# First column of the first projection: two weight tiles times the first 528 tokens in plain fp32, tile by tile as the rows come

## The reference

```python
h = rms_norm(x, norm_pre[0])              # 1056 tokens x 1024
proj = h @ w_in[0]                        # 1024 -> 4 * 1024
v, bg, cg, z = jnp.split(proj, 4, axis=-1)
u = cg * v
conv = w_conv[0] * u_ext[:, 0:T] + ...    # three taps over time
y = (bg * conv * jax.nn.silu(z)) @ w_out[0]
x = x + rms_norm(y, norm_post[0])
```

## Time and profile before

| | us |
|---|---|
| median of 3 runs | 1091.33 |
| lowest, highest | 1090.86, 1092.24 |
| the profiled execution | 1090.71 |
| its span, first to last instruction | 1089.0 |

### The profile page before, as it was taken

How to read it: one execution, slowest core, us unless ns; L and a number is a source line. 1 busy time by engine, 2 the same in 40 slices (tenths; PEclk the granted TensorE clock), 3 DMA queues, 4 the chain that set the end, 5 groups by cost and what they waited for, 6 DMA issues and landing times.

```text
span 1089.0 us, 20411 instructions
## 1 busy us (share of the span) xinstructions
PE 1066.0 (98%) x7995; PEld 1002.6 (92%) x7995; DVE 723.7 (66%) x1294; ACT 386.5 (35%) x738; POOL 38.8 (4%) x53
## 2 busy tenths in 40 slices
PE   6999999999999999999999999999999999989997
PEld 6999999999999888799999999999999999967885
DVE  6798677677678546645657495875849587485146
ACT  7443333333335344433142331414233241532123
POOL 1000000000000000001001010100101010010000
PEclk9999999999999999999999999999999999999999
DMA  6102221211121542122202211210221121121143
GB/s 223 38 20 78 58 60 39 57 58 39 58 58 58 168 144 98 64 64 58 59 23 59 61 48 48 60 55 25 58 60 41 56 60 46 54 77 60 42 178 121
DMA packets 93317, 74.30 MB, mean 68 GB/s; under 512 B 2519, under 2 KB 85528, under 8 KB 93274
## 3 DMA queue, kind: packets, MB, share of 16 engines
q1 hardware_dynamic: 75482, 64.80, 19.1%
q10 hardware_dynamic: 17792, 8.91, 2.8%
HBM read 60.26 MB, written 13.44 MB: 68 GB/s over the span
## 4 chain that ended last, share of the span: by engine, by line
PE 90%; DVE 6%; DMA 2%; issue 1%; ACT 0%; SPq 0%; DVEq 0%; ACTq 0%
PE bank L560 34%; PE bank L608 23%; PE bank L707 16%; PE bank L580 2%; PE bank L781 2%; PE bank L775 2%; DMA wraw<-in_w_in 1%; PE bank L827 1%; PE bank L851 1%; PE bank L858 1%; PE bank L860 1%; PE bank L812 1%; PE bank L722 1%; PE bank L688 1%; PE bank L684 1%
## 5 line engine op out<-in xcount | busy, mean ns | idle before, releaser
L560 PE MATMUL bank<-reg_a,wsplit 128*128 128x352 f32 x2304 | 388.0, 326 | 0.6 <-ACT arena L1228 0.6
L560 PEld LDWEIGHTS bank<-reg_a,wsplit 128*128 128x128 f32 x2304 | 368.4, 188 | 3.3 <-issue 0.9
L608 PE MATMUL bank<-reg_a,wsplit 128*128 128x264 f32 x1344 | 165.5, 284 | 0.0
L608 PEld LDWEIGHTS bank<-reg_a,wsplit 128*128 128x128 f32 x1344 | 164.1, 188 | 0.1
L608 PE MATMUL bank<-reg_b,w_ring 128*128 128x264 f32 x1008 | 124.7, 284 | 0.4 <-DVE wraw L1542 0.4
L608 PEld LDWEIGHTS bank<-reg_b,w_ring 128*128 128x128 f32 x1008 | 123.3, 188 | 0.6 <-DVE wraw L1542 0.6
L707 PE MATMUL bank<-reg_a,reg_b 128*128 128x512 f32 x288 | 69.9, 396 | 1.0 <-DVE reg_a L1420 1.0
L707 PE MATMUL bank<-reg_b,reg_a 128*128 128x512 f32 x288 | 68.7, 395 | 0.0
L707 PEld LDWEIGHTS bank<-reg_a,reg_b 128*128 128x128 f32 x288 | 53.8, 188 | 14.2 <-DVE reg_a L1420 1.7
L707 PEld LDWEIGHTS bank<-reg_b,reg_a 128*128 128x128 f32 x288 | 53.9, 188 | 12.6
L1608 DVE TENSOR_TENSOR arena<-arena,bank 128x264 f32<-128x264 f32 x84 | 34.7, 426 | 33.5 <-PE bank L608 32.3
(11 more groups left out here) (260 smaller groups left out, 1515.2 us busy)
## 6 DMA issues: line engine op xcount, KB each, us to landing
wraw<-in_w_in SPq DMA_DIRECT2D x64, 512.0 KB, 4.1
arena<-in_x_prompt SPq DMA_DIRECT2D x16, 512.0 KB, 3.7
wraw<-in_w_out SPq DMA_DIRECT2D x16, 512.0 KB, 3.3
x_scratch<-arena SPq DMA_DIRECT2D x8, 512.0 KB, 2.6
arena<-in_state_hgrn ACTq DMA_DIRECT2D x8, 512.0 KB, 3.9
out<-arena ACTq DMA_DIRECT2D x8, 512.0 KB, 3.0
arena<-x_scratch SPq DMA_DIRECT2D x8, 512.0 KB, 3.3
out<-arena SPq DMA_DIRECT2D x7, 512.0 KB, 2.7
```

The costliest lines, as they stand in the source:

```text
L560: mm = nc.tensor.matmul(bank[b][:, 0:CH], w[wi][:, k, :], rhs[hi], start=(k == 0 and i == 0), stop=(k == KT - 1 and i == 2))
L608: mm = nc.tensor.matmul(bank[banks[q]][:, 0:QT], w[wi][:, k, :], B_OP[name][hi][:, k, q * QT:(q + 1) * QT], start=(start and k == 0 and i ...
```

## The change

Groups 0 to 3 (tiles 0 and 1 times the first two token ranges) are no longer made of three fast products of split operands. A new function `plain_rows(t, i)` multiplies weight tile t as loaded (`wraw`) by row tile i as weighed (`h_raw`), eight matmuls of plain fp32 into the same bank; two row tiles fill one bank. The token ranges are cut at 0, 256, 528, 768 and 1056 instead of every 264 tokens, so that the first two end near tile borders: row tile 3's piece has 144 columns and also needs row tile 4.

What follows from it in the order of the engines: SP issues the two weight loads directly behind row tiles 0 and 1, in the stream ahead of tile 1 and tile 2, and the loads of weight tiles 2 and 3 wait for the plain products that read `wraw`. PE makes one plain piece between two turned tiles. ACT and DVE split ranges 2 and 3 first and ranges 0 and 1 last (`SPLIT_ORDER`), which groups 8 and up read. `keep_busy` stands ahead of the first transposes (15 and 4), no longer between the tiles. The wait for the two small DVE steps moved from tile 0 to tile 1.

```diff
+QE = (0, 256, 528, 768, T)
+SPLIT_ORDER = (2, 3, 0, 1)
...
                 if i:
                     load_input(i)
-                if i == 3:
-                    load_w(0, wsrc(w_in[0], 0), 0, 0, False)
-                if i == 4:
-                    load_w(1, wsrc(w_in[0], 2 * D), 1, 0, False)
+                if i < 2:
+                    load_w(i, wsrc(w_in[0], i * 2 * D), i, 0, False)
...
             for t in (2, 3):
+                sp.wait_ge(proj_done, t + 1)
                 load_w(t, wsrc(w_in[0], COL0[t]), t % 2, 1)
...
             pe.wait_ge(pool_ev.sem, pool_ev.at(0, "id"))
+            keep_busy(15)
             pe.wait_ge(vec_in, 5 * 16)
...
             mm.then_inc(K_PE, 1)
-            pe.wait_ge(K_DVE, 2)
+            keep_busy(4)
...
-                pe.wait_ge(S_LO.sem, S_LO.at(q, "lo"))
+                pe.wait_ge(S_LO.sem, S_LO.at(SPLIT_ORDER.index(q), "lo"))
                 w = slot(t % 2)
-                cols = slice(q % 2 * QT, (q % 2 + 1) * QT)
+                cols = slice(QE[q] - q // 2 * HT, QE[q + 1] - q // 2 * HT)
...
-            BETWEEN = {2: 12, 3: 8, 4: 8}
-            START = {4: 0, 5: 1, 6: 2, 7: 3, 8: 4}
-            for i in range(TT):
-                turn_input(i)
-                if i in BETWEEN:
-                    keep_busy(BETWEEN[i])
-                if i in START:
-                    first_group(START[i])
+            def plain_rows(t, i):
+
+                q = i // 2
+                b = J0_BANK[2 * q + t]
+                first, end = i * P, QE[q + 1] if i % 2 else (i + 1) * P
+                if i % 2 == 0:
+                    pe.wait_ge(bank_free[2 * q + t], emptied(0))
+                pe.wait_ge(w_in_s[t], 16)
+                pe.wait_ge(S_DT.sem, S_DT.at((end - 1) // P, "tb"))
+                for k in range(KT):
+                    mm = nc.tensor.matmul(bank[b][:, first - QE[q]:end - QE[q]], wraw[:, t, k, :], h_raw[:, k, first:end],
+                                          start=(k == 0), stop=(k == KT - 1))
+                if i % 2:
+                    mm.then_inc(proj_done, 1)
...
+            turn_input(0)
+            plain_rows(0, 0)
+            plain_rows(1, 0)
+            turn_input(1)
+            plain_rows(0, 1)
+            turn_input(2)
+            plain_rows(1, 1)
...
+            turn_input(6)
+            plain_rows(1, 3)
+            turn_input(7)
+            first_group(4)
+            turn_input(8)
             for g in range(5, 4 * NQ):
                 first_group(g)
...
-                act.wait_ge(S_DT.sem, S_DT.at((2, 4, 6, 8)[q], "tb"))
+                act.wait_ge(S_DT.sem, S_DT.at((QE[q + 1] - 1) // P, "tb"))
...
+            for i in range(5):
+                normalise(i)
+            first_hi(0)
+            normalise(5)
+            first_hi(1)
+            normalise(6)
+            first_v(0)
+            normalise(7)
+            token_hi(2)
+            normalise(8)
+            first_v(1)
+            token_hi(3)
+            token_hi(0)
+            token_hi(1)
             act.wait_ge(K_DVE, 3)
...
+            for i in range(4):
+                weigh(i)
+                normalise(i + 1)
+            normalise(5)
+            weigh(4)
+            first_lo(0)
+            normalise(6)
+            weigh(5)
+            first_u(0)
+            token_lo(2)
+            normalise(7)
+            weigh(6)
+            first_lo(1)
+            normalise(8)
+            weigh(7)
+            weigh(8)
             token_lo(3)
             first_u(1)
+            token_lo(0)
+            token_lo(1)
             dve.wait_ge(K_ACT, 1)
```

More of the change, by code:

```diff
@@ L525, in _, with keep_busy @@
         def _(pe):
+            def keep_busy(n):
+                for k in range(n):
+                    nc.tensor.transpose(bank[0][:, 0:P], ident[:, :], ident[:, :])
             pe.wait_ge(pool_ev.sem, pool_ev.at(0, "id"))
+            keep_busy(15)
             pe.wait_ge(vec_in, 5 * 16)
@@ L1009, in first_v @@
                 b = (0, 2)[q % 2]
-                a, e = q * QT, min((q + 1) * QT, NP)
+                a, e = QE[q], min(QE[q + 1], NP)
                 ins = A(c_u[:, 2 + a:2 + e], bank[b][:, 0:e - a], ACT.Copy)
                 if q == NQ - 1:
-                    ins = A(us[:, :, 2:], bank[b][:, e - a:QT].rearrange("p (b s) -> p b s", b=NB), ACT.Copy)
+                    ins = A(us[:, :, 2:], bank[b][:, e - a:T - a].rearrange("p (b s) -> p b s", b=NB), ACT.Copy)
                 ins.then_inc(bank_free[b], 1)
@@ L1017, in _ @@
             A(small[:, 47:48], eps[:, :], ACT.Sqrt)
-            normalise(0)
-            normalise(1)
-            for i in range(9):
-                if i + 2 < TT:
-                    normalise(i + 2)
-                if i == 1:
-                    first_hi(0)
-                if i == 3:
-                    first_hi(1)
-                if i in (2, 4, 6, 8):
-                    token_hi(i // 2 - 1)
-                if i == 6:
-                    first_v(0)
-                if i == 8:
-                    first_v(1)
+            for i in range(5):
[12 more added lines that the diff above has]
+            token_hi(1)
             act.wait_ge(K_DVE, 3)
@@ L1071, in _ @@
                 act.wait_ge(proj_done, 3 * NQ + q + 1)
-                A(c_gate[:, q * QT:(q + 1) * QT], bank[J0_BANK[q]][:, 0:QT], ACT.Sigmoid).then_inc(F_ACT.now(f"g{q}"), 1)
+                A(c_gate[:, QE[q]:QE[q + 1]], bank[J0_BANK[q]][:, 0:QE[q + 1] - QE[q]], ACT.Sigmoid).then_inc(F_ACT.now(f"g{q}"), 1)
             for name in PRODUCTS[2:]:
@@ L1470, in first_lo, with weigh @@
                                 ALU.subtract).then_inc(w_lo, 1)
-            normalise(0)
-            for i in range(9):
-                r = P if i < 8 else NSAMP
-                if i < 8:
-                    normalise(i + 1)
+            def weigh(i):
+                r = rows_of(i)
                 for half, name in enumerate(("ta", "tb")):
@@ L1570, in _ @@
                 dve.wait_ge(proj_done, 2 * NQ + q + 1)
-                cols = slice(q * QT, (q + 1) * QT)
-                V.tensor_tensor(c_acc[:, cols], bank[J0_BANK[q]][:, 0:QT], c_acc[:, cols], ALU.mult).then_inc(bank_free[q], 1)
+                cols = slice(QE[q], QE[q + 1])
+                V.tensor_tensor(c_acc[:, cols], bank[J0_BANK[q]][:, 0:QE[q + 1] - QE[q]], c_acc[:, cols], ALU.mult).then_inc(bank_free[q], 1)
             dve.wait_ge(T_DVE.sem, T_DVE.at(0, "t3"))
```

46 lines of the change are left out of this document (23 added, 23 removed).

## The result

The changed kernel is slower by 0.29%. That is over the mark of 0.2% that the prediction took, though the lower end of the interval (0.19%) lies just under it.

What follows compares the result with a forecast made beforehand. Up to about 48 us, DVE's work and its round trips with PE were taken to bind, PE behind; +2.0 us on the 1091.33 us median gave 1093.3 us, range 1091.6 to 1096.6.

Steps and rivals of the forecast that it cites:

- Where the time is decided: Near 48 us: weight tile 2's low part and product 8 start late by 2.0 to 2.1 us; everything behind moves along.
- pass through: From 48.3 to 104.5 us DVE's order is unchanged, so the 2.0 us delay arrives behind it.
- The plain product: On PE, 1.78 us per 128-token piece; all eight pieces 14.7 us against 11.8, 2.9 us more work.
- The loads: Four early transfers at 352 to 370 GB/s: weights 0 land at 9.5, tile 1 at 10.7, weights 1 at 11.4.
- The walk: Step-by-step schedule from tile 0 to product 8: tile 1 turned at 13.4, product 8 at 50.5; chance 0.54.
- rival 1: At the start, loads land in issue order: first piece 8.8, tile 1 turned 12.4; +1.0 us, 1092.3; chance 0.17.
- the landing of weights 1: At the start, weight tile 1 arrives at 11.4 us, range 11.0 to 12.0, and holds back tile 1's turning.
- Even if the plain pieces behind tile 1 cost nothing: Early tiles: free pieces would save about 0.9 us only, since PE-DVE round trips set the pace from tile 2.
- Rival 2: First two plain pieces run at half clock, 3.56 us each, tile 1 turned at 16.7; +5.3 us, 1096.6; chance 0.15.
- rival 3: Up to product 8, PE binds and not DVE, with tile 1 turned at 10.6; -4.3 us, 1087.0; chance 0.07.
- rival 4: Between 48 and 104 us, DVE stops and a load swallow the delay; 0 us, 1091.3; chance 0.07.
- the term for product 8: Near 50 us, the delay of product 8's start that is carried to the end, booked as +2.0 us.

Runs made afterwards that it cites:

- e4: The changed kernel with four of the eight matmuls of every plain piece left out; 1094.99 us, ratio 1.0038 to the kernel before.
- e1: The changed kernel with DVE normalising one tile ahead and PE turning the next tile ahead of the plain piece, from tile 2 on; 1091.19 us, ratio 1.0001.
- e5: e1 with tiles 7 and 8 turned and weighed ahead of product 4, some DVE and ACT split steps reordered; 1088.51 us, ratio 0.9975.
- e11: e5 with weight tile 1's load behind tile 2's and its first plain piece behind tile 1's turning; 1087.92 us, ratio 0.9973.
- e12: The changed kernel with only DVE's half of e1's reordering, PE's order as in the change; 1094.36 us, ratio 1.0028.
- e2: The changed kernel with token range 1's split moved behind weight tile 2's low part, range 0's high part also moved; 1095.96 us, ratio 1.0055.
- e3: The changed kernel with the loads of weight tiles 0 and 1 back behind row tiles 3 and 4; 1098.60 us, ratio 1.0074.
- e7: e3 with 40 identity transposes filling PE between tile 0's turning and the first plain piece; 1098.68 us, ratio 1.0070.
- e8: The changed kernel without the 15 and 4 leading identity transposes ahead of tile 0; 1095.72 us, ratio 1.0045.

## Why the prediction was right or wrong

The time was in the range: 1094.03 against 1093.3, range 1091.6 to 1096.6. But I gave "no change" 0.53 and "slower" 0.40, and it is slower past the mark. That the time came within 0.7 us is in part luck: my +2.0 us stood on a median of 1091.33, and beside the changed kernel the kernel before had 1090.86. The change was worth +2.5 us in the traces and +3.2 in the medians.

- **Where the time is decided: right.** Weight tile 2's low part and product 8 were named as the two starts that matter; they are 2.78 and 2.76 us late, and 2.50 us arrive in the last column's products. The step "pass through" held; the stop of 0.4 us at 104.48 was its only slack, and I had not booked it as such.
- **The plain product: right.** A piece takes 1.86 us from its start to that of the tile behind it (12.04 to 13.90, 15.97 to 17.83), a later one 1.79 (24.49 to 26.28); 1.78 was predicted. The clock under them in the profiled run wasn't the loss, and behind tile 2 their arithmetic wasn't either (e4).
- **The loads: mechanism right, size short.** Weight tile 0 was there at 8.9 (9.5 predicted), tile 1 at 10.2 (10.7), weight tile 1 at about 12.0 (11.4). The walk's first half microsecond is made here: tile 1 turned at 13.90 and not 13.4. The rate of 352 to 370 GB/s was right once it flowed (355 GB/s from 8 to 12), but from 4 to 8 only 204 GB/s moved, against 262 before. That is 0.23 MB less, which at 355 GB/s is 0.65 us, by an estimate about what weight tile 1 was late by; why the start was slower stays open. What waited for the four transfers started in the order of issue (8.96, 10.21, about 12.0, 13.25), as in rival 1. The Trainium skill, "DMA: Bandwidth & Descriptors", section "Queues, rings and completion order", has each DMA engine consume the descriptors of a queue in ring order, but it says too that completion is not in that order for certain, so that the landings one after the other were my inference and not the page's. The order did not make it faster: rival 1's first piece at 8.8 came true (8.96), its tile 1 at 12.4 did not, because weight tile 1 was there only at about 12.0. The term that failed here is the landing of weights 1.
- **The walk: right in form.** The stops before tile 7, product 6 and product 8 and DVE's run without a stop from 41 on are all there, each 0.7 to 1.0 us later than in the walk: tile 7 at 34.13 (33.3), product 6 at 43.91 (42.9), the low part at 49.85 (49.1), product 8 at 51.16 (50.5). PE's stops ahead of product 6 and product 8 are shorter than predicted, 2.49 and 0.62 us for some 3 and 1. The stops at tile 7 and product 6 were not seen as places where the clock can fall.
- **"Even if the plain pieces behind tile 1 cost nothing, the walk would shorten by about 0.9 us only": right in direction, wrong in reach.** e4 took half of them out and had 1.6 us by tile 7, nothing at the end. But the sentence hid that the round trips which "set the pace" are a matter of two orders: e1 changes nothing else and takes off 2.3 us.
- **Rival 2, the clock: right in kind, wrong in place.** The first pieces ran at full speed in the profiled run in part at half speed in e5 (5.47 us for 32 records) and at half speed in e11 (3.73 for 16). What the changed kernel pays by it lies, as far as can be inferred, at product 6.
- **Rivals 3 and 4.** PE did not come to bind; with tiles first it nearly does (in e5 its one stop behind 17.3 is the 0.62 us ahead of product 8), 2 us ahead of the kernel before: of rival 3's 4.3 us, which assumed tile 1 turned at 10.59 and no cost on DVE, e5 and e11 have 2.2 and 2.5 at product 8. Of rival 4, 0.26 us of 2.76 were swallowed.

The sum was mis-sized by the term for product 8 (2.0, measured 2.76, of which 2.50 arrive) and by leaving out the clock at product 6 (about 0.6 us, seen in e12).

## What to carry to other kernels

When work moves from one engine to another, write down for each tile who is ahead of whom in both queues. Here two orders that each look harmless (weigh, then normalise the next; a piece, then turn the next) form a chain together: undoing DVE's alone gave nothing, undoing both gave 2.3 us, and PE's alone wasn't run. A split that must be done anyway has to be booked where it goes, not only where it leaves: the end moves only when the busy engine's stops go away. And a stop of PE can have a price beyond its own length: here one of 2.5 us did in five of eight executions, those of 4.17 and 4.82 us both times.

## What the hardware showed

- With the same 19 transposes ahead of it, tile 0's turning took 1.09 us in the changed kernel, e2 and e3 but 1.91 or 1.92 in e1, e4, e5, e7, e11 and e12. So PE is at full speed before 7 us in some executions and only behind 10 us in others, with the same work ahead of it. The Trainium skill ("TensorE: Matmul & The Clock Gate", Part 1) has the throttled state as the default that activity releases, and warns that the number of slow matmuls at the start differs between runs of one kernel; the runs agree on both (without the 19 transposes, in e8, tile 0's turning took 1.97 us).
- After a stop of 2.5 us the clock fell in five of eight profiled executions that had it and not in the others; after 4.17 and 4.82 us it fell both times (24 records in 4.44 us instead of 2.93; 32 records in 6.37 us instead of 3.74). After the stop of 4.36 us shortly before 970 us it was low in all fourteen (0.97 or 0.93 on average from 950 to 1000), but for different times. The stretch table prints it (0.62 in 44 to 48), while tiles turned at half speed before 14 us stand beside a printed 1.00. Why the clock fell in five and not in three, no run shows.
